# Two norms moved inside projections, and the first product tile moved into the first norm's stage

## What is computed

```python
h = rms_norm(x, attn_norm_g);  u = h @ w_in              # 1024 x 2048
# pooling of u's first 512 columns, rotary on q and k, differential attention of 4 heads
x = x + concat(y_pool, y_diff) @ w_out                   # output projection, 1024 x 1024
# cross attention with mem, 256 rows of width 1024
q  = rms_norm(x,   xattn_norm_g) @ w_cq                  # 1024 x 1024
kv = rms_norm(mem, mem_norm_g)  @ w_ckv                  # 1024 x 2048
x = x + softmax(q k^T / 16) v @ w_co
# then 32 experts, top 4, and the second block, which the change does not touch
```

## Time and profile before

| | us |
|---|---|
| runs | 2853.45, 2856.04, 2862.97 (median 2856.04) |
| profiled execution | 2850.96 |
| its span in the trace | 2849.2 |
| PE busy | 2635.1 (92%) |
| VectorE busy | 1881.7 (66%) |
| ScalarE busy | 1432.4 (50%) |
| GpSimd busy | 633.3 (22%) |
| moved by transfers | 595.89 MB, mean 209 GB/s |

### The profile page before, as it was taken

One profiled execution on the slowest core, in us unless ns is written; L12 is line 12 of the kernel. 1 busy time (PEld: TensorE's weight loads), 2 busy tenths in 40 slices (PEclk: granted clock), 3 DMA queues, 4 the chain that ended last, 5 costly groups with the idle time before them and its releaser, 6 DMA issues. The chain is left out here.

```text
span 2849.2 us, 44654 instructions
## 1 busy us (share of the span) xinstructions
PE 2635.1 (92%) x18026; PEld 2160.9 (76%) x18026; DVE 1881.7 (66%) x1864; ACT 1432.4 (50%) x1517; POOL 633.3 (22%) x247
## 2 busy tenths in 40 slices
PE   7988887999999999999999979979789799899998
PEld 6768757788888888888888748756488677888887
DVE  5574345899999999999999843447845533422234
ACT  4342333677777777777777642335434222522222
POOL 0003001444444444444444220000043000000000
PEclk9989998999999999999999989989999899999999
DMA  5343222899999999999999853331010223122221
GB/s 190 121 148 130 89 69 100 338 384 383 382 382 383 384 382 383 381 384 384 383 383 383 334 210 118 143 112 52 12 40 4 76 111 109 70 104 92 101 90 44
DMA packets 112279, 595.89 MB, mean 209 GB/s; under 512 B 12144, under 2 KB 13936, under 8 KB 65200
## 3 DMA queue, kind: packets, MB, share of 16 engines
q1 hardware_dynamic: 95200, 538.74, 48.2%
q0 software_dynamic: 7056, 25.69, 2.9%
q10 hardware_dynamic: 9888, 29.50, 2.7%
HBM read 568.72 MB, written 25.17 MB: 208 GB/s over the span
## 5 line engine op out<-in xcount | busy, mean ns | idle before, releaser
L1210 DVE TENSOR_TENSOR weights_low<-weight_ring,weights_high 128x2048 fp32r<-128x2048 f32 x384 | 865.5, 2285 | 54.5 <-ACT weights_high L1156 54.5
L1156 ACT CAST weights_high<-weight_ring 128x2048 fp32r<-128x2048 f32 x384 | 726.7, 1909 | 179.6 <-PE psum L1065 145.5
L1025 POOL TENSOR_SCALAR rank_onehot<-iota,members 128x128 bf16<-128x128 f32 x132 | 444.9, 3380 | 1.0 <-issue 0.2
L351 DVE TENSOR_TENSOR w_low<-weight_ring,w_high 128x2048 fp32r<-128x2048 f32 (+1 forms) x92 | 213.1, 2317 | 330.5 <-ACT w_high L346 330.1
L346 ACT CAST w_high<-weight_ring 128x2048 fp32r<-128x2048 f32 (+1 forms) x86 | 162.6, 1891 | 283.6 <-PE psum L378 143.6
L1065 PE MATMUL psum<-weights_high,expert_x_high 128*128 128x512 f32 x1024 | 278.5, 394 | 2.9 <-DVE expert_x_low L1214 2.9
L1065 PE MATMUL psum<-weights_low,expert_x_high 128*128 128x512 f32 x1024 | 274.6, 390 | 0.0
L1065 PE MATMUL psum<-weights_high,expert_x_low 128*128 128x512 f32 x1024 | 273.9, 390 | 0.0
L1019 POOL DMA_INDIRECT expert_x<-hidden,index x33 | 89.7, 2718 | 782.6 <-DVE index L1205 589.5
L1065 PEld LDWEIGHTS psum<-weights_low,expert_x_high 128*128 128x128 f32 x1024 | 192.9, 188 | 40.2
L1065 PEld LDWEIGHTS psum<-weights_high,expert_x_low 128*128 128x128 f32 x1024 | 192.6, 188 | 39.9
(11 more groups left out here) (539 smaller groups left out, 4953.7 us busy)
## 6 DMA issues: line engine op xcount, KB each, us to landing
weight_ring<-in_w_gu SPq DMA_DIRECT2D x256, 1024.0 KB, 8.9
weight_ring<-in_w_down SPq DMA_DIRECT2D x128, 1024.0 KB, 8.9
weight_ring<-in_w_in SPq DMA_DIRECT2D x35, 1024.0 KB, 4.9
weight_ring<-in_w_ada SPq DMA_DIRECT2D x24, 1024.0 KB, 4.8
weight_ring<-in_w_ffn_in SPq DMA_DIRECT2D x22, 1024.0 KB, 4.8
expert_table<-expert_y ACTq DMA_DIRECT2D x32, 512.0 KB, 9.3
weight_ring<-in_w_ffn_out SPq DMA_DIRECT2D x11, 1024.0 KB, 4.8
weight_ring<-in_w_out SPq DMA_DIRECT2D x8, 1024.0 KB, 4.9
```

What stands on the lines that cost most here:

```text
L351: self.m.nc.vector.tensor_tensor(low, w, high.bitcast(F32), ALU.subtract).then_inc(self.ready.sem, 1)
L1025: last = nc.gpsimd.tensor_scalar(oc[:, t, :], iota[:, :], members[:, t, e], None, ALU.is_equal)
L1156: nc.scalar.copy(high[:, n % 4, :], slot(n)).then_inc(rounded.sem, 1)
L1210: V.tensor_tensor(low[:, n % 4, :], slot(n), high[:, n % 4, :].bitcast(F32), ALU.subtract).then_inc(ready.sem, 1)
```

## The change

**First tile.** `first_norm` also makes tile 0 of unit 0, in the order high by high, high by low of x, low of the weights by high; each product waits for the part that it reads. It goes to bank 0, once bank 0's low part has been read. VectorE makes the low parts of x ahead of the differences of units 0 and 1, and ScalarE casts unit 1 behind its high parts. `project_first` starts with tile 1; VectorE's difference of unit 2 stands ahead of the rotary tables.

**Memory's norm** is made in `add_projection`: squares behind ScalarE's first cast, the root behind its second, the scaling behind the seventh added tile, 16 transposes into banks 4 to 7 behind the third unit, high and low parts beside the fourth, and at last the parts of the first unit of `memory_kv`. The projection's tiles keep banks 0 to 3. The load of `mem` is first on SyncE's queue.

**The norm of x** is made in `memory_kv`. The squares go between ScalarE's copies, and the scale is ready at the fifth unit. x is not scaled by itself: ScalarE makes four diagonal matrices (the identity times each token's scale), and an f32 product of an x block with such a matrix transposes and scales at once. 16 such products stand behind the fifth unit, 16 behind the seventh, into banks 4 to 7. The three bias loads are issued behind the cast of unit 1.

Both `norm` stages are gone. `Split`, `split_tile` and `project_to` work as before, the weight parts have fixed places through the three stages.

```diff
@@ project_first
-            for u in range(6):
+            split_tile(m, first, x, KD, 1, 1).then_inc(done.sem, 1)
+            for u in range(1, 6):
@@ add_projection, PE
-                    if i >= 8:
-                        pe.wait_ge(freed.sem, freed.at(i - 7))
-                    split_token_tile(m, w, x, KD, t, i % 8, t == 0).then_inc(done.sem, 1)
+                    if i >= 4:
+                        pe.wait_ge(freed.sem, freed.at(i - 3))
+                    split_token_tile(m, w, x, KD, t, i % 4, t == 0).then_inc(done.sem, 1)
+                if u == 2:
+                    pe.wait_ge(scaled.sem, scaled.at(MT))
+                    for k in range(KD):
+                        for t in range(MT):
+                            last = nc.tensor.transpose(turns(k)[:, t * P:(t + 1) * P], xn[:, t, k * P:(k + 1) * P], m.ident[:, :])
+                        if k % 2:
+                            last.then_inc(turned.sem, 1)
@@ add_projection, ScalarE
-            for u in range(1, 4):
-                split.round(act, u)
+            split.round(act, 1)
+            act.wait_ge(fetched.sem, fetched.at(16))
+            for t in range(MT):
+                nc.scalar.activation(xn[:, t, :], mem[:, t, :], ACT.Square, scale=1.0 / 32, accum_out=stat[:, 0, t:t + 1]).then_inc(squares.sem, 1)
+            split.round(act, 2)
+            act.wait_ge(mean.sem, mean.at(1))
+            nc.scalar.activation(stat[:, 2, 0:MT], stat[:, 1, 0:MT], ACT.Sqrt).then_inc(root.sem, 1)
+            split.round(act, 3)
+            for b in range(KD // 2):
+                act.wait_ge(turned.sem, turned.at(b + 1))
+                for k in (2 * b, 2 * b + 1):
+                    last = nc.scalar.activation(high[:, k, :], turns(k), ACT.Identity, scale=scale[:, k:k + 1])
+                last.then_inc(rounded.sem, 1)
+            act.wait_ge(done.sem, done.at(12))
+            ahead.round(act, 0)
@@ memory_kv, PE
+            def turn(g):
+                pe.wait_ge(scaled.sem, scaled.at(NT))
+                if g:
+                    pe.wait_ge(parted.sem, parted.at(4))
+                for k in range(4):
+                    for t in range(NT):
+                        last = nc.tensor.matmul(ps[4 + k][:, t * P:(t + 1) * P], m.X[:, t, (4 * g + k) * P:(4 * g + k + 1) * P],
+                                                turner[:, t, :], start=True, stop=True)
+                    last.then_inc(turned.sem, 1)
 
             for u in range(8):
                 w = split.take(pe, KD)
-                if u >= 4:
-                    pe.wait_ge(freed.sem, freed.at(2 * u - 6))
+                if u >= 2:
+                    pe.wait_ge(freed.sem, freed.at(2 * u - 2))
...
+                if u in (4, 6):
+                    turn(u // 2 - 2)
@@ memory_kv, ScalarE, ahead of the copy of tile i
                 if i % 2 == 0 and i < 14:
                     split.round(act, i // 2 + 1)
+                if i == 0:
+                    biases.load(act)
+                if i in (1, 3, 5, 7):
...
+                    nc.scalar.activation(sink[:, :], m.X[:, t, :], ACT.Square, scale=1.0 / 32, accum_out=stat[:, 0, t:t + 1]).then_inc(squares.sem, 1)
+                if i == 8:
+                    act.wait_ge(mean.sem, mean.at(1))
+                    nc.scalar.activation(stat[:, 2, :], stat[:, 1, :], ACT.Sqrt).then_inc(root.sem, 1)
+                    act.wait_ge(mean.sem, mean.at(2))
+                    for t in range(NT):
+                        nc.scalar.activation(turner[:, t, :], m.ident[:, :], ACT.Copy, scale=stat[:, 3, t:t + 1]).then_inc(scaled.sem, 1)
+                if i == 10:
+                    high_parts(0)
+                if i == 14:
+                    act.wait_ge(done.sem, done.at(14))
+                    ahead.round(act, 0)
+                    high_parts(1)
@@ memory_kv, VectorE
-            for u in range(1, 8):
-                split.rest(dve, u)
+            for u in range(1, 5):
+                split.rest(dve, u)
+            dve.wait_ge(squares.sem, squares.at(NT))
+            V.tensor_scalar(stat[:, 1, :], stat[:, 0, :], EPS1, None, ALU.add).then_inc(mean.sem, 1)
+            dve.wait_ge(root.sem, root.at(1))
+            V.reciprocal(stat[:, 3, :], stat[:, 2, :]).then_inc(mean.sem, 1)
+            for u in (5, 6):
+                split.rest(dve, u)
+            low_parts(0)
+            split.rest(dve, 7)
+            ahead.rest(dve, 0)
+            low_parts(1)
@@ first_norm, PE
+            w_high, w_low = split.take(pe, KD, wait=False)
+            out, tile = ps[0][:, :], slice(0, P)
+            pe.wait_ge(split.rounded.sem, split.rounded.at(1))
+            pe.wait_ge(parted.sem, parted.at(1))
+            for k in range(KD):
+                pe.wait_ge(rounded.sem, rounded.at(k + 1))
+                nc.tensor.matmul(out, w_high[:, k, tile], high[:, k, :], start=(k == 0), stop=False)
+            for k in range(KD):
+                pe.wait_ge(parted.sem, parted.at(k + 1))
+                nc.tensor.matmul(out, w_high[:, k, tile], low[:, k, :], start=False, stop=False)
+            pe.wait_ge(split.ready.sem, split.ready.at(1))
+            for k in range(KD):
+                last = nc.tensor.matmul(out, w_low[:, k, tile], high[:, k, :], start=False, stop=(k == KD - 1))
+            last.then_inc(done.sem, 1)
```

More of the change, by code:

```diff
@@ L358, in head, with take @@
         self.rest(dve, 0)
-    def take(self, pe, k, cols=UC):
+    def take(self, pe, k, cols=UC, wait=True):
         ring = self.m.ring
@@ L365, in take @@
         ring.next_use += 1
-        pe.wait_ge(self.ready.sem, self.ready.at(i + 1))
+        if wait:
+            pe.wait_ge(self.ready.sem, self.ready.at(i + 1))
         shape = lambda z: z[:, 0:k * cols].rearrange("p (k n) -> p k n", k=k)
@@ L389, in split_tiles, with project_first @@
         split_tile(m, w, x, ktiles, j, (i + j) % banks, n).then_inc(done.sem, 1)
-def project_first(m, x, split, up, qk, v, y, tabs):
+def project_first(m, x, split, first, up, qk, v, y, tabs):
     nc, ps = m.nc, m.ps
@@ L408, in _ @@
         def _(sp):
-            m.ring.load(sp, 8)
+            m.ring.load(sp, 7)
         @block.tensor
@@ L693, in diff_attention, with add_projection @@
     turned_out.end(N), made.end(N), out_copied.end(N), os_.end(2 + DH), squared.end(N), oturn.end(DH)
-def add_projection(m, x, split, fetch=None):
+def add_projection(m, x, split, mem, xn, memT, stat, scale, weights):
     nc, ps = m.nc, m.ps
-    done, freed, fetched = stage_signals(m, "tile_done", "tile_freed", "tokens_loaded")
+    done, freed, fetched, squares, mean, root, scaled, turned, rounded = stage_signals(
+        m, "tile_done", "tile_freed", "tokens_loaded", "norm_squares", "norm_mean", "norm_root", "norm_scaled", "norm_turned",
+        "norm_rounded")
+    split.end(4)
+    ahead = Split(m, weights, ahead=4)
+    high, low = memT
+    turns = lambda k: ps[4 + k // 2][:, k % 2 * MEM:(k % 2 + 1) * MEM]
     with nc.Block() as block:
@@ L760, in _, with high_parts @@
         def _(act):
-            biases.load(act)
+            def high_parts(g):
+                for k in range(4 * g, 4 * g + 4):
+                    act.wait_ge(turned.sem, turned.at(k + 1))
+                    nc.scalar.activation(high[:, k, :], ps[4 + k % 4][:, :], ACT.Identity, scale=scale[:, k:k + 1]).then_inc(rounded.sem, 1)
             for i in range(16):
@@ L769, in _, with low_parts @@
         @block.vector
         def _(dve):
-            for u in range(1, 8):
-                split.rest(dve, u)
-    split.end(8), done.end(16), freed.end(16)
+            V = nc.vector
+            def low_parts(g):
+                for k in range(4 * g, 4 * g + 4):
+                    dve.wait_ge(rounded.sem, rounded.at(k + 1))
+                    V.scalar_tensor_tensor(low[:, k, :], ps[4 + k % 4][:, :], scale[:, k:k + 1], high[:, k, :].bitcast(F32),
+                                           ALU.mult, ALU.subtract).then_inc(parted.sem, 1)
@@ L776, in project_to @@
+            low_parts(1)
+    done.end(16), freed.end(16), squares.end(NT), mean.end(2), root.end(1), scaled.end(NT), turned.end(KD), rounded.end(KD), parted.end(KD)
+    return ahead
 def project_to(m, x, split, dst, tiles):
@@ L3398, in first_norm @@
     high, low = parts
-    loaded, row_loaded, step, exps, squares, mean, root, scaled, turned, rounded = stage_signals(
+    loaded, row_loaded, step, exps, squares, mean, root, scaled, turned, rounded, parted, done = stage_signals(
         m, "loaded", "row_loaded", "small_step", "small_exp", "norm_squares", "norm_mean", "norm_root", "norm_scaled", "norm_turned",
-        "norm_rounded")
+        "norm_rounded", "x_parted", "tile_done")
+    first = []
     fetched = [Signal(m, f"x_fetched{t}") for t in range(NT)]
@@ L3507, in program @@
                 with ExitStack() as st3:
-                    first_norm(m, st3, xn, x, m.col("attn_norm_g", 0, 8), split, neglam[:, :])
```

(8 more changed lines are left out.)

80 lines of the change are left out of this document (57 added, 23 removed).

## The result

The changed kernel took 2831.92 us (median of 2831.62, 2831.92 and 2834.42) against 2856.04: a ratio of 0.9913 with a 95% interval of 0.9884 to 0.9942. That is 24 us faster; the forecast was 2828.5, in a range of 2819 to 2841.

A forecast was written before the change was run, and what follows sets the result against it. PE was taken to bound the projections, with idle norms and half-clock restarts between them. Gains of 4.0 + 11.0 + 12.35 = 27.4 us off the 2856.04 median gave 2828.6, stated as 2828.5; range 2819 to 2841.

The forecast's parts named there:

- the turning: In memory_kv, 32 f32 products that transpose and scale x: 64 records at 0.11 us, 7.1 us added on PE.
- Part 1: First tile made in the first norm's stage: second tile's copy 3.3 to 5.0 us earlier, taken as 4.0.
- Part 2: Memory's norm inside the output projection: 12.75 us taken away, 1.8 added for 16 transposes, net 11.0.
- Out plus gap 1: From the output projection's first add to memory's first copy, where a net gain of 11.0 us was claimed.
- Part 3: Norm of x inside the memory projections: 19.45 us taken away, 7.1 added for turning x, net 12.35.
- kv plus gap 2: From memory's first copy to q's first copy, where a net gain of 12.35 us was claimed.
- the handover of units: In memory_kv, copy, cast and difference take 5.9 us against 5.76; late in the old trace too, and "this stays".
- Gap 2: From memory's last copy to q's first: 25.56 us before; copy, boundary and warm tile, together 6.1, after.
- The rule against it: Transposes don't count as clock activity, so 16 in the output projection act as a pause: 1.5 us; rival 8%.
- Cold turning: Rival, 14%, with late handovers: added PE work at half clock or units late; gain 17, time 2839.
- The split stayed in the shadow: Against a 3% rival: in memory_kv casts and differences come wholly behind products, net 20 us slower, 2876.
- taken back in the experts' stage: Rival, 4%: the experts' start has a time of its own, all 27 us waited out there, time 2855.

The follow-up runs named there:

- e5: The changed kernel with each group of 16 f32 turning products issued twice into the same banks; 2836.91 us in one run.
- e3: The changed kernel with the norm of x a stage of its own again, behind the old memory_kv; 2842.11 us, ratio 0.9956 to the kernel before.
- e4: The changed kernel with the split of the experts' biases (loads and GpSimd's instructions) moved from memory_kv into project_to; 2831.33 us, ratio 0.9914 to the kernel before.
- e7: The changed kernel with the bias split moved into project_to and x scaled first, then turned by 32 transposes; 2827.43 us, ratio 0.9902 to the kernel before.

## Why the prediction was right, and where it was off

The mechanism was as forecast: two norms with their cold restarts left PE's path, PE got the turning in exchange, and the shift reached the experts whole. 27.4 us were forecast; the stages of the first pair of traces give 4.2 + 10.9 + 11.2 = 26.3.

*Part 1*: forecast 4.0 between 3.3 and 5.0, measured 4.2. The open point was whether products with pauses keep the clock; they did, and by the forecast's own working that is worth 5.0. The start of the high parts at 16.25, 0.7 later than before, took back what that gave; counted from that start the gain is 4.7 to 4.9 over all traces. So the 4.0, taken between the two cases, was 0.7 to 0.9 too low, and the 4.2 is close to it by chance.

*Part 2*: forecast 11.0. Out plus gap 1 went from 59.7 to 48.8, so 10.9. The 16 transposes take 1.91 in the trace and delay the next add by 1.7 (forecast 1.8), nothing else in the output projection became late, and memory's load was there at 195.4.

*Part 3*: forecast 12.35, measured 11.2 (kv plus gap 2 from 69.46 to 58.25). The turning was sized right, 7.1 against 7.2 by e5. The term that was mis-sized is the handover of units: I wrote that its lateness "stays". Sixteen tiles 2.88 apart make 43.2 from the first to the last copy; before they took 43.9, late by 0.7, and the changed kernel 51.8 - 7.1 - 43.2 = 1.5. The cold start used to cover it, but not by letting the weights' parts get ahead: the difference for the fourth unit starts 10.84 us behind the first copy before, and 10.85 after. What moved is GpSimd's first subtraction. From the start of the stage to the first copy it is 4.5 us cold and 3.2 warm, and the bias loads land 8.2 us after their issue before, 9.3 in the changed kernel and 8.4 in e3; so the subtraction ends 12.2 us behind the first copy before, and 13.3 in the changed kernel and in e3. The difference, held until then, ends 1.1 us later, and PE waits 1.2 us for it. Since e3 has this without part 3, the lateness belongs to part 2, which warmed the start; e4 shows that it goes with GpSimd's work, while that the shift of that work made it grow is read from these rows and tested by no run of its own. I had noted that differences take up to 3.62 beside GpSimd, but carried that length over as if it did not depend on when the two meet. Gap 2 was 6.4 against 6.1 forecast.

*The rule against it* would have cost 1.5 us behind the transposes. The granted clock is 1.00 from 226.60 to 240.00, and in e7 through both groups, so that price was not paid. The Trainium skill ("TensorE: Matmul & The Clock Gate", Part 4) says that transposes don't count as activity. These groups last 1.9 us each and are a weak test of it, since PE also kept the clock through a true pause of 1.21 us; what speaks against it in this case is the rise of the clock within transposes alone.

*The other rivals.* Cold turning did not come: memory_kv has clock 1.00 throughout. The split stayed in the shadow but for one unit, so one of the forecast's signs of being wrong did come: PE idle in memory_kv for a weight difference, 1.2 us. Nothing was taken back in the experts' stage, from its first to its last product with `weights_high` and `expert_x_high` 1122.3 us before and 1122.1 to 1124.1 after.

*The number*: medians give 24, not 27.4. With three runs on each side the interval allows 17 to 33; the two later comparisons give ratios of 0.9904 and 0.9894, 27 and 30 us, and medians 25.8 and 27.9 apart. The range took in the spread of the runs, but not a late part that varies by 7.7 us between two traces of the kernel before and by 9.1 between two of the changed one. That the time still fell well inside was luck in part.

## What to carry to other kernels

Price a norm between two projections by the distance between the last copy of the one and the first of the other, restart at half clock included: that gave 16.4 and 25.6 us here, and what was left after the move, a boundary and a warm tile, could be predicted within 0.4. When a cold start goes, look at what runs beside PE by a time of its own, here the bias split that begins when its loads land: it meets the other engines' work at another point than in the old trace, and an instruction's length read there doesn't carry over. And for an edit of 5 us in a program whose own late stages vary by 8 to 9, read the stage, not the total.

## What was not expected of the hardware

A VectorE instruction on 128x4 values took 4.08 us while GpSimd worked, against 0.16 in e4; a difference of 2.29 took up to 4.62. The rows fit one engine waiting for the whole instruction of the other: the lengthened differences end 2.1 to 2.2 us behind a GpSimd instruction, the tiny one 0.03 behind. A tiny instruction on the chain of a norm can thus cost as much as a large one.

PE kept clock 1.00 through pauses of 0.84 and 1.21 us between groups of products in the first tile, and through groups of 16 transposes of 1.91 us.

Two traces of one program differ by 7.7 us behind the experts' first product; in one stretch the granted clock was 0.89 in one and 0.81 in the other, and the stretch took 41.7 and 45.2 us.
